# Experts that gather from x, a top four by match and replace, and eight once-filled weight slots

## The reference

```python
x = x + gate1 * mixed
h2 = rms_norm_2(x, norm2_g) * (1.0 + scale2) + shift2      # 256 x 1024
logits = h2 @ w_router + b_router                          # 32 experts
top_val, top_idx = lax.top_k(logits, 4)
gates = softmax(top_val)
# for each expert e, over the tokens that chose it:
gu = h2[tokens] @ w_gate_up[e] + b_gate_up[e]              # 1024 x 2048
g = minimum(gu[:, :1024], 7); u = clip(gu[:, 1024:], -7, 7)
y = ((u + 1) * (g * sigmoid(1.702 * g))) @ w_down[e] + b_down[e]   # 1024 x 1024
out = x + gate2 * (sum over the token's four experts of gate * y)
```

## Time and profile before

| | |
|---|---|
| median of three runs | 2289.99 us |
| the profiled execution | 2289.59 us |
| its span | 2287.7 us |
| PE busy | 2192.6 us (96%) |
| DVE busy | 972.4 us (43%) |
| ACT busy | 618.8 us (27%) |
| main DMA queue | 632.49 MB |
| granted TensorE clock, mean | 0.998 |

### The profile page before, as it was taken

The page is one execution under the profiler, slowest core; times in us unless marked ns, Lnnn a source line. Parts: engine busy times, 40 slices in busy tenths (PEclk is TensorE's granted clock), DMA queues, the critical chain, the costliest instruction groups (busy, mean ns, idle before and its releaser), DMA issues. The chain is left out here.

```text
span 2287.7 us, 29587 instructions
## 1 busy us (share of the span) xinstructions
PE 2192.6 (96%) x12171; PEld 1322.1 (58%) x12172; DVE 972.4 (43%) x1400; ACT 618.8 (27%) x842; POOL 91.0 (4%) x137
## 2 busy tenths in 40 slices
PE   8999989999999999899999989999999999999998
PEld 7886865788788866758887753333333333333332
DVE  4663574566575537646548761111111111111111
ACT  4432332544344232234335641010000000101000
POOL 5000020000000000200001000000000000000000
PEclk9999999999999999999999999999999999999999
DMA  8763321776387442147854569999999999999998
GB/s 303 236 242 97 131 75 38 232 264 223 109 291 250 159 142 75 39 129 254 279 184 133 185 261 413 428 429 428 429 428 429 428 429 409 429 428 429 428 429 357
DMA packets 190785, 633.88 MB, mean 277 GB/s; under 512 B 29728, under 2 KB 126000, under 8 KB 164064
## 3 DMA queue, kind: packets, MB, share of 16 engines
q1 hardware_dynamic: 190688, 632.49, 71.8%
HBM read 631.38 MB, written 1.07 MB: 276 GB/s over the span
## 5 line engine op out<-in xcount | busy, mean ns | idle before, releaser
L409 PE MATMUL banks<-ffn_room 128*128 128x512 f32 x1920 | 453.7, 392 | 0.0
L409 PEld LDWEIGHTS banks<-ffn_room 128*128 128x128 f32 x1920 | 357.5, 188 | 72.8
L526 DVE TENSOR_TENSOR ffn_room<-memory,ffn_room 128x2048 fp32r<-128x2048 f32 x124 | 280.9, 2290 | 100.6 <-ACT ffn_room L486 100.6
L2952 DVE TENSOR_SCALAR attend_words<-banks 128x512 f32<-128x512 f32 x32 | 22.1, 691 | 571.3 <-PE banks L2749 571.3
L486 ACT CAST ffn_room<-memory 128x2048 fp32r<-128x2048 f32 x124 | 232.5, 1904 | 72.2 <-PE banks L427 61.8
L427 PE MATMUL banks<-ffn_room 128*128 128x512 f32 x1056 | 248.2, 390 | 0.3
L2749 PE MATMUL banks<-memory,attend_words 128*64 128x512 f32 x1040 | 229.8, 593 | 0.0
L427 PEld LDWEIGHTS banks<-ffn_room 128*128 128x128 f32 x1056 | 197.6, 188 | 42.8 <-DVE ffn_room L565 2.1
L2749 PE MATMUL banks<-attend_later,attend_words 128*64 128x512 f32 x720 | 162.8, 600 | 0.1
L2749 PEld LDWEIGHTS banks<-memory,attend_words 128*64 128x64 f32 x1040 | 71.9, 135 | 147.4 <-issue 138.6
L2769 PE MATMUL banks<-memory,attend_words 128*64 128x512 f32 x512 | 116.9, 596 | 14.9 <-DMA memory<-in_w_down 14.9
(11 more groups left out here) (443 smaller groups left out, 2490.8 us busy)
## 6 DMA issues: line engine op xcount, KB each, us to landing
memory<-in_ffn_w SPq DMA_DIRECT2D x132, 1024.0 KB, 7.5
memory<-in_w_gate_up SPq DMA_DIRECT2D x59, 2048.0 KB, 23.4
attend_later<-in_w_gate_up SPq DMA_DIRECT2D x41, 2048.0 KB, 23.2
memory<-in_w_down SPq DMA_DIRECT2D x29, 2048.0 KB, 25.4
attend_later<-in_w_down SPq DMA_DIRECT2D x17, 2048.0 KB, 25.5
attend_words<-in_w_gate_up SPq DMA_DIRECT2D x17, 2048.0 KB, 24.8
memory<-in_w_in SPq DMA_DIRECT2D x32, 1024.0 KB, 6.0
memory<-in_w_ada SPq DMA_DIRECT2D x32, 768.0 KB, 5.6
```

Source lines behind the costliest of these rows:

```text
L409: m = nc.tensor.matmul(psum[:, GU + tt, :], x_parts[:, xp, k, tt * P:tt * P + P], rows, start=(n == 0), stop=(n == 3 * KD - 1))
L526: tt_op(b, chip.ring[:, chip.slot(base + i), :], a.bitcast(F32), ALU.subtract).then_inc(chip.used, 1)
L2952: ts(room.gate, psum[:, GATE_BANK, :], 7.0, None, ALU.min).then_inc(s["g_ready"], 1)
```

## The change

Five parts. **The experts gather from x**: `h2` is no longer made. The selection matrix holds 1/rms of the token instead of 1 (`routed.scaled`), so that the gather gives normed rows, and gain and shift are put on when the turned rows are copied into `xeT`, one instruction for each of the eight blocks of 64 columns. For expert 0 DVE does four of the eight. **The top four** come from MAX8, `match_replace` with a mark, and a comparison. **New x** is made for token tile 0, then for each half of tile 1, and output blocks 6 and 7 are ordered for that; the **router** is turned and multiplied by halves. The **gates**' sum, division and turn move into `experts_phase`, as does the load of `b_down`; the four adds of x to the sums (`add_x`) are spread, and most fills are left out. **Eight slots** are filled once: tiles 2 and 3 of expert 19 join; seven are issued in `attend_phase`, each when its place is free.

```diff
-EXTRA, APART = 6, 18
+EXTRA, APART = 8, 18
-FREE_EARLY = 3
+FREE_EARLY = 7
...
+            thin += [(dst.rearrange("p (j c) -> p j c", c=2), by_pair(src)) for dst, src in
+                     ((routed.gainT, norm2[0:1, :]), (routed.scaleT, mod_row[0:1, 4 * D:5 * D]),
+                      (routed.shiftT, mod_row[0:1, 3 * D:4 * D]))]
...
             for m in range(RING, 2 * RING - 1):
                 ...
-            chip.issue(sp, loads, OUT + RING, OUT + N_OUT + RING)
+            once(0)
+            once(1)
+            chip.issue(sp, loads, OUT + RING, OUT + RING + 2)
             sp.wait_ge(s["pv"], ALL)
             ...
+            once(2)
+            once(3)
+            chip.issue(sp, loads, OUT + RING + 2, OUT + RING + 3)
+            sp.wait_ge(s["mixT"], 1 + STEPS)
+            once(4)
+            chip.issue(sp, loads, OUT + RING + 3, OUT + RING + N_OUT)
+            sp.wait_ge(s["n_ss"], NT)
+            once(5)
+            sp.wait_ge(s["r_mm"], 1)
+            once(6)
...
+            new_x(0, slice(0, D), s["mixed"], 1)
+            new_x(1, slice(0, D // 2), s["mixed"], 2)
+            new_x(1, slice(D // 2, D), chip.used, OUT + N_OUT)
...
+            turn_x(0, 0)
+            turn_x(0, 1)
+            pe.wait_ge(s["shifted"], 1)
+            mm(psum[:, 1, 0:NE], room.ones, room.cst, start=True, stop=True).then_inc(s["cst_mm"], 1)
+            turn_x(1, 0)
+            pe.wait_ge(s["hT_last"], 1)
+            logits(0, 0)
+            turn_x(1, 1)
+            logits(0, 1)
+            logits(1, 0)
+            logits(1, 1).then_inc(s["r_mm"], 1)
...
+            ts(st[:, 10:10 + NT], hst[:, 0:16:8], -1.0, None, ALU.mult)
+            chain(nc.vector.memset(top[:, :, TOP:8], ABSENT))
+            dve.wait_ge(s["pchain"], POOL_ALL)
+                m = nc.vector.match_replace(room.marked[:, tt, :], top[:, tt, :], logit[:, tt, :], MARK)
+            chain(m)
+            ts(routed.chosen[:, :, 0:NE], room.marked[:, :, 0:NE], MARK, None, ALU.is_equal).then_inc(s["rank"], 1)
+            dve.wait_ge(s["rank"], 1)
+            tt_op(routed.scaled[:, :, 0:NE], routed.chosen[:, :, 0:NE], each_col(st[:, 4:4 + NT], NE), ALU.mult)
...
             def take_gathered(e):
                 act.wait_ge(s["rows_turned"], e + 2)
-                copy(room.xeT.rearrange("p (h c) n -> p c h n", h=2),
-                     psum[:, SHARED_BANK, :].rearrange("p (c h n) -> p c h n", c=4, h=2)).then_inc(s["xe"], 1)
+                for c in range(2 if outside(e) else 4):
+                    for h in range(2):
+                        k = 4 * h + c
+                        m = nc.scalar.activation(room.xeT[:, k, :], psum[:, SHARED_BANK, c * P + CAP * h:c * P + CAP * h + CAP],
+                                                 ACT.Identity, bias=routed.shiftT[:, k:k + 1], scale=routed.gainT[:, k:k + 1])
+                m.then_inc(s["xe"], 1)
...
             with act.Fori(1, NE - 1) as e:
                 take_back(e)
                 take_rows(e)
+                sigmoid(e)
                 take_gathered(e)
-                sigmoid(e)
                 take_hidden(e)
```

More of the change, by code:

```diff
@@ L1598, in __init__ @@
         self.place = w.take(chip.NT * (NE + 1)).rearrange("p (t e) -> p t e", t=chip.NT)
+        self.scaled = w.take(chip.NT * (NE + 1)).rearrange("p (t e) -> p t e", t=chip.NT)
+        self.gainT, self.shiftT, self.scaleT = (w.take(chip.KD) for _ in range(3))
         self.counts = w.take(NE)
@@ L1662, in __init__ @@
         self.split = w.take(SPLIT_WORDS).rearrange("p (s q n) -> p s q n", s=4, q=2)
-        D = chip.D
-        self.gate1, self.shift2, self.scale2, self.b_down = (later[:, i * D:i * D + D] for i in range(4))
+        self.gate1 = self.b_down = chip.norm_gb[:, 0, :]
         w = Words(words, 0, words.shape[1])
@@ L1919, in output @@
                 for tt in tts:
-                    for half in range(2):
+                    for half in parts:
                         m = mm(psum[:, 2 * tt + half, :], chip.xT[:, k, tt * P:tt * P + P],
                                part[:, k % 2, half * 512:half * 512 + 512], start=(k == 0), stop=(k == KD - 1))
-                    if tt == 0 and k == KD - 1:
+                    if k == KD - 1 and not (tt and parts[-1]):
                         m.then_inc(s["mixed"], 1)
-                if k % 2 and tts[-1] == 1:
+                if k % 2 and tts[-1] == 1 and parts[-1] == 1:
                     m.then_inc(chip.used, 1)
@@ new lines, in _, with turn_x @@
+            output(7, (0,))
+            output(7, (1,), (0,))
+            output(6, (1,), (1,))
+            output(7, (1,), (1,))
+            def turn_x(tt, h):
+                pe.wait_ge(s["x_new"], 1 if tt == 0 else 2 + h)
+                for k in range(4 * h, 4 * h + 4):
+                    m = nc.tensor.transpose(psum[:, 4 + 2 * tt + h, (k % 4) * P:(k % 4) * P + P],
+                                            chip.x[:, tt, k * P:k * P + P], ident)
+                m.then_inc(s["x_turned"], 1)
@@ new lines, in logits @@
+            def logits(tt, h):
+                pe.wait_ge(s["hT_last" if h else "hT_first"], tt + 1)
+                for k in range(4 * h, 4 * h + 4):
+                    m = mm(psum[:, 4, tt * NE:tt * NE + NE], chip.xT[:, k, tt * P:tt * P + P], room.wr[:, k, :],
+                           start=(k == 0), stop=(k == KD - 1), skip_group_check=True)
+                return m
+            turn_x(0, 0)
+            turn_x(0, 1)
+            pe.wait_ge(s["shifted"], 1)
+            mm(psum[:, 1, 0:NE], room.ones, room.cst, start=True, stop=True).then_inc(s["cst_mm"], 1)
@@ L2020, in _ @@
                 .then_inc(s["route_mm"], 1)
[L2022 to L2027 removed]
+            add_x(chip, 0, 1)
         @block.scalar
@@ L2503 @@
 ACC, GATE_BANK, UP_BANK, Y_BANK, SHARED_BANK = 0, 4, 5, 6, 7
-EXPERTS = ("picked gu_read g_ready sig gated hidden sel back back_turned back_out gathered rows_out rows_turned xe "
+EXPERTS = ("gates tables_turned gatesT down_rows xe_low chain picked gu_read g_ready sig gated hidden sel back back_turned back_out gathered rows_out rows_turned xe "
            "turned act ye scat last_half down_bias tables scat_first first_rows last_rows")
@@ L3075, in _ @@
             act.wait_ge(s["l_gathered"], 1)
-            for b in range(2):
-                m = copy(room.xeT[:, 4 * b:4 * b + 4, :], psum[:, 6 + b, :].rearrange("p (k n) -> p k n", k=4))
+            for k in range(KD):
+                m = nc.scalar.activation(room.xeT[:, k, :], psum[:, 6 + k // 4, (k % 4) * P:(k % 4) * P + P], ACT.Identity,
+                                         bias=routed.shiftT[:, k:k + 1], scale=routed.gainT[:, k:k + 1])
             m.then_inc(s["l_xeT"], 1)
@@ L3096, in _ @@
             for tt in range(NT):
+                ts(room.rows_of_e[:, tt, :], room.places[:, ds1(half), :].rearrange("p a n -> p (a n)"), routed.place[:, tt, ds1(e)],
+                   routed.scaled[:, tt, ds1(e)], ALU.is_equal, ALU.mult)
                 m = ts(room.sel[:, tt, :], room.places[:, ds1(half), :].rearrange("p a n -> p (a n)"), routed.place[:, tt, ds1(e)],
```

201 lines of the change are left out of this document (95 added, 106 removed).

## The result

| | before | change |
|---|---|---|
| median of 20 runs, us | 2292.12 | 2295.27 |
| lowest to highest | 2287.87 to 2294.55 | 2290.91 to 2300.17 |
| profiled execution, its span | 2289.59, 2287.7 | 2296.45, 2294.8 |
| mean granted clock of the profiled span | 0.998 | 0.992 |

The ratio is 1.0014 with a 95% interval of 1.0008 to 1.0021: slower by 3.2 us, where 2284.9 was forecast (a gain of 0.2%). The time lies above my range of 2281.5 to 2290.0.

A forecast was written before the change was run, and what follows sets the result against it. The weight stream at 428 GB/s was taken to bound the experts, so its start sets the end: 2289.59 - 5.7 (head) + 0.65 (first turn) - 0 (slots) = 2284.5, plus 0.4 for the median, 2284.9; range 2281.5 to 2290.0.

The forecast's parts named there:

- Gain in the head 5.7: Attention's output to expert 0's bias pick: the pick comes at 1365.3 instead of 1370.97, 5.7 us earlier.
- First turn: Expert 1's turn: sigmoid, then eight activations; lag 2.1 us against the stream's reserve of 1.4, a 0.65 us gap.
- rival D: PE's clock falls to the 1.2 GHz level from router to tile 1: +13.3 us, 2298; chance 12%.
- New x by halves: After output block 6: DVE starts new x 1.7 us earlier; x complete at 1350.3 instead of 1351.7.
- Router by halves: Router matmuls: end at 1355.55 instead of 1356.6, gain 1.05 us; logits start at 1355.7.
- Top four: DVE, logits to rank: 1.9 us instead of 4.07, match-and-replace pair taken at 0.6; rank at 1357.6.
- Gather to pick: Expert 0's gather to bias pick: 3.95 us before, plus 0.1, 0.1 and 0.3; gather 1360.7, pick 1365.3.
- Activations of 64 columns: ScalarE's copies of gathered blocks: 0.23 us each by a straight line, four 0.9, eight 1.85.
- Two slots worth 0: Stream about expert 19: 4.9 us less transfer, but the hole grows from 2.5 to about 7.4 us; worth 0.
- Expert periods: Experts once PE has caught up with the weights: the same 29.36 us each, set by DMA.

The follow-up runs named there:

- e8: The change plus fills in the head, expert 1's copies shared by DVE and ScalarE, early pick and `b_down` adds, last x turns before the router: 2285.09 us, 0.9979 of before.
- e1: The change plus one group of three fills in TensorE's idle stretch ahead of the first router matmuls: 2291.37 us, 1.0008 of before.
- e2: The change plus fills in each TensorE wait from the last output block to the rank: 2290.12 us, 0.9996 of before.
- e10: The kernel before without its fills around the turns of x and of the gates, and one instead of two before the first gather: 2297.53 us, 1.0023 of before.
- e11: The change plus fills in the head's waits (as e2) and six fills in TensorE's wait ahead of expert 1: 2290.10 us, 0.9995 of before.
- e4: The change with six once-filled slots instead of eight, all issued before the experts begin: 2295.84 us, 1.0020 of before.
- e7: e2 plus expert 1's eight copies shared by DVE and ScalarE ahead of the sigmoid, its bias pick made before them: 2289.56 us, 0.9993 of before.
- e9: e8 with six once-filled slots instead of eight: 2289.55 us, 0.9990 of before.
- e12: e8 with DVE reading expert 0's sums first, then doing two of the eight copies, ScalarE six: 2286.81 us, 0.9981 of before.

## Why the prediction was wrong

The step that failed is the first term of the sum, **"Gain in the head 5.7"**. It priced every matmul at full clock. In the profile the clock fell to half just after the router's first matmuls and stayed there for some 17 us, and the head grew by 1.4 us: 7.1 off the forecast. A second term was mis-sized in the same direction: the first turn lost 3.7 us of the stream instead of "+0.65". What failed in the head is answered by rival D's mechanism, in its place (router, counts, adds, gather at half clock), which I gave 12%; its price there was 13.3 us, 4.8 of them for the turns, the pick and two tiles, which ran at full clock again, so the 8.5 left of it are what compares with the 7.1. At full clock the size of the term was right: e8's head is 5.68 shorter than before's. e1, e2 and e10 show the cause: fills put into the waits take 5.5 and 5.6 us off the change's head, and leaving them out of the kernel before adds 3.4 to its own.

My reason against D was that 1305 to 1365 ran at 1.00 with its waits. That row was of a kernel with fills in those waits; it says what clock the fills keep and nothing of the clock without them. Nor was the drop at 1880 the only one in that profile: 0.77 and 0.89 stand over 10 to 15 and 15 to 20. The Trainium skill's rule ("TensorE: Matmul & The Clock Gate", The HAM clock gate), that the clock goes by how busy TensorE has recently been, made D the likelier case; the traces agree in direction (0.53 over 1354 to 1372, e10 0.57 over 1360 to 1368), and I set it aside for a row that didn't bear on it. Why the clock then stayed down while PE was busy 17.70 of 18 us, the traces don't show.

Point by point:

- *New x by halves*: right. x was complete at 1352.66, 9.99 us after block 6's start, where the forecast amounts to 9.99.
- *Router by halves*: forecast, the logits start at 1355.7, 15.4 us after block 6 (1340.31 in that profile). They start 18.3 after it: the last 24 instructions took 5.17 us instead of 2.8. In e8, at full clock and with its other order, it is 1358.86 - 1343.52 = 15.3.
- *Top four*: right, 1.63 us against my 1.9; the pair of match-and-replace at 0.42 against 0.6.
- *Gather to pick*: a slip in the sum. 1360.7 + 3.95 + 0.5 is 1365.15, not 1365.3, so the terms as listed give 5.8, not 5.7.
- *Activations of 64 columns*: mis-sized. 0.31 each (2.45 for eight, 1.29 for four) against my 0.23. The straight line through 128 and 512 columns doesn't go on below 128: 64 columns (0.31) are no cheaper than 128 (0.28). By an estimate from the Trainium skill's budget ("ScalarE: Activation LUTs", Rules for kernel authors), about 0.3 us and 0.83 ns per element, one of 64 columns takes 0.35, nearer to the measured 0.31 than my line.
- *First turn*: the term was +0.65 us (a lag of 2.1, a reserve of 1.4). Measured is a lag of 4.2 and a loss of 3.7. e11, the same turn with the clock held, has 29.47: so 2.6 of the lag are the wait, which is my 2.1 and 0.6 for the dearer activations, and 1.6 are clock (a pick of 1.22 instead of 0.72, and 4.78 instead of 3.65 behind it). The reserve was mis-sized too: in e8, where the turn came 1.9 later than before's with the clock at 1.00, the stream lost 1.7 us, and in e11 2.6 cost 2.0. So hardly any of the 1.4 was there, and my lag of 2.1 would have cost some 1.6 us, within the bounds of 0 and 2 but not 0.65.
- *Two slots worth 0*, hole 7.4 us, ended by a later pair: the hole is 7.4 us, and SP is silent for 23.7 us ahead of the pair that ends it (1904.89 to 1928.63, the last two of the three issues in 27.50 us), as the forecast has it (1897.74 to 1921.48). The worth of 0 is right as far as e4 can tell.
- *Expert periods*: unchanged, chain 2102.80 to 2132.08, 29.3 us.
- *The margin*: the median came out 3.2 above before, less than the profile's 7.1 - 2.4 = 4.7. Executions differ in how long the clock is down, as the clusters near 2291, 2295 and 2300 of the 20 runs suggest.

Left open: what exactly makes the clock fall. In the change and in e10 it fell after 1.70 and 1.16 us of idle time and a run of 32-column matmuls, in e2, e7, e9, e11 and e12 after 0.40 or 0.41 of idle time and such a run. The same run left the clock at 1.00 in before (0.21 of idle time, behind fills) and in e1 and e8 (0.41). So neither the run nor the short wait decides it alone. e8 held its clock with the turns ahead of the router; e9 and e12, with the same code there, dipped (0.66 over 1357 to 1362, 0.57 over 1357 to 1361), so that order is no cure. The difference between e8's and e2's ratio, 3.9 us, isn't split between the order, the sharing and the smaller hole either.

## What to carry to other kernels

Before an edit takes matmuls, fills above all, out of a stretch in which PE waits, price the stretch at half clock, and read the clock over many runs, since one profile is one draw. A queue of prefetched tiles saves time only if the consumer frees the next slots before the queue is out: look at which read frees each slot, and move a short independent piece of work out of that interval. An engine's share taken off a critical turn needs the order of its other work looked at too, or the wait only changes its releaser.

## What the runs showed of the hardware

- The granted clock differs between executions of one kernel whose instructions are the same: 0.995 to 1.000 in 98 runs of before, with times of 2287.3 to 2295.4. A straight line through the clock takes up a bit under half of this spread; the rest isn't explained.
- A fall need not end with the work that follows: in the change PE was busy 17.70 of 18 us at 0.53 before the clock came back.
- A match-and-replace over 128x36 takes 0.18 us and its value load 0.09, two in 0.42.
- A table load of 1.28 us ran in ScalarE's idle time, ahead of the wait for its operand (1385.36, with the sigmoid at 1392.37).
